# First norm carried into the matmuls, first mixer: compression panels between the dense ones, gates beside the values

## The chip, the cores and the metric

One core of one Trainium2 chip. The metric is the time of one execution on the device in microseconds, median of several runs. One run was also profiled, and all rows below come from it.

## What is computed

Two transformer blocks over 512 tokens of 1024 features, in float32. The change touches only the front of the first block: the first norm and the projections that feed its mixer.

```
h = rms_norm(x, norm_mix_pre)             # x * rsqrt(mean(x*x) + eps) * w, over 1024 features
proj = h @ w_in                           # 1024 -> 2840 columns, split into
rq, rk (256 each), rv, rg (512 each)      # retention: 4 heads, chunks of 128
nq (512), kcm, vcm (128 each)             # sparse attention: queries, and what is compressed
ksl, vsl, kwn, vwn (128 each), ng (24)    # selected and window keys and values, mixing gates
y_ret = silu(rg) * groupnorm(retention(rope(rq), rope(rk), rv))
# compress(): 31 overlapping blocks of 32 tokens, + pos_emb, flattened to 2048
kc = gelu(blocks(kcm) @ cmp_k_w1) @ cmp_k_w2        # 2048 -> 256 -> 64; the same for vc
out = sigmoid(ng)-weighted sum of attention over kc/vc, selected and window keys
x = x + rms_norm(concat(y_ret, out) @ w_out, norm_mix_post)
```

The matrix products are made from split operands: a float32 weight or activation becomes a rounded high part and the remainder, and each product is three matmuls (high by high, low by high, high by low).

## The kernel before

**Panels.** All weights come as panels of 128 x 1024 floats (512 KB), numbered in the order of use. `SP` loads panel p into `raw[p % 4]` as soon as the low part of panel p-4 exists. ScalarE makes the high part (`split`, a copy of 128 x 1024 into `w_hi[p % 2]`, line 1195), VectorE the remainder (`low`, line 1753, into `w_lo[p % 2]`). `split(p)` waits until TensorE has read panel p-2 (`panel_read`), so behind each panel that TensorE finishes there is a chain of one `split` and one `low` before the panel after next can start. `dense` (lines 489 to 491 through `product`) takes one panel: 8 tiles of three matmuls with 512 moving columns, 24 matmuls. `token_major` takes four panels and puts tokens on the partitions: 96 matmuls.

**Order by hand.** Each engine's program is one list, written out by hand and joined by semaphores. In the front TensorE runs: the sums of squares of the norm (`norm_sums`, line 532), the spread of the inverse root (`norm_wide`, line 549), then panels `RET_Q`, `RET_K` (4 dense), `RET_V` (4, token major, 512 wide), `RET_G` (4 dense), `CMP_IN` (2), `NSA_Q` (4), `NSA_K` (2), `NSA_V` (4, token major, 256 wide), `NSA_GATE` (1 panel of 32 stationary columns, 24 matmuls of 512), `CMP_W1` (8 panels, 12 matmuls of 256 each with 62 stationary columns), `CMP_W2` (1). Then the attention part begins: `best_round` (line 646), 18 rounds whose maxima VectorE takes (`largest`, line 2122), and `block_scores` (line 667). The pieces of the retention (`ret_scores`, `ret_values` line 615, `ret_sums` line 621) are put between tiles of dense panels.

**The first norm.** `x` comes in one DMA on ScalarE's queue, behind two others. ScalarE squares the 8 tiles, VectorE adds them up, TensorE sums over partitions, GpSimd takes the power, VectorE spreads it on a diagonal, TensorE widens it, and only then VectorE scales tile after tile (line 1821), ScalarE makes the high part (line 1289) and VectorE the low part (line 1828) for the first dense panel. Later norms of the kernel are "carried": the matmuls run on x times the gain, and the inverse root multiplies the results.

**VectorE's helpers in the front.** `rope_panel` (lines 1953 to 1958, four operations of 128 x 512), `ret_decay` (line 1997), the centring of the values (lines 2023 to 2025), `xg` building for the compression (line 2044, eight operations for each of keys and values), `xg_low` (line 2030), `q_lows` (line 1976), `k_lows` (line 1984). All sit in one queue with `low`.

Of the kernel before, what the change touches and what calls it, by code (L numbers as in the profile page):

```python
# [21 lines left out]
P = 128  # L22
# [12 lines left out]
FF0 = 42  # L35
# [64 lines left out]
CARRIED = ("ffn_pre", "ab", "ffn1", "c", "ffn2")  # L100
# [14 lines left out]

def output_of(panel):

    before = panel - sum(4 for at in (RET_V, NSA_V, AB_V, AB_VB, AB_O) if panel > at)
    return before if panel <= CMP_W1 else before - 2 if panel <= MLA_V else before - 2 - 2 - PAIRS


CMP_O = output_of(CMP_W1)


def bank_at(panel):

    if AB_U <= panel < AB_O:
# [11 lines left out]
def build_in(nc, A, ctx):  # L139
# [25 lines left out]
    with ExitStack() as c:  # L165
# [83 lines left out]
    def table(t, where, name):  # L249
# [4 lines left out]
    consts_in, x_in, first_in, second_in, pos_in = (sem(n) for n in (  # L254
        "consts_in", "x_in", "first_in", "second_in", "pos_in"))
# [5 lines left out]
    gates_turned, cmp_in_ready, cmp_turned, cmp_ready, v_ready = (sem(n) for n in (  # L261
        "gates_turned", "cmp_in_ready", "cmp_turned", "cmp_ready", "v_ready"))
# [34 lines left out]


# [52 lines left out]
    inv_b = tmp[:, 1, :]  # L351
    ADDED = ("ffn_pre", "ab")
# [26 lines left out]
    def _(sp):  # L379
        for n in range(4):  # L380
# [13 lines left out]
    def _(pool):  # L394
# [7 lines left out]
        pool.wait_ge(consts_in, 32)  # L402
        sets = [6]
# [28 lines left out]
        pool.wait_ge(x_in, 32)  # L432
# [53 lines left out]
    def _(pe):  # L486
# [6 lines left out]
        def w(panel, a, b):  # L493
            return w_hi[:, panel % 2, a:b], w_lo[:, panel % 2, a:b]

        def dense(panel, i=None, moving=(h_hi, h_lo), tiles=KD, ready=None, base=0, most=None, between=None, freed=False):
# [298 lines left out]
        pe.wait_ge(consts_in, 32)  # L795
        pe.wait_ge(x_in, 16)
        norm("mix_pre")
        pe.wait_ge(pool_set, 6)
# [17 lines left out]

        def retention_in(panel):
            def between(k):
                if k in ret_work[panel]:
                    part, n = ret_work[panel][k]  # L820
                    part(n)
            return between if panel in ret_work else None

        for panel in range(RET_G, NSA_V):
            dense(panel, between=retention_in(panel))
        pe.wait_ge(ret_p, 16)
        pe.wait_ge(ret_ms, 4)
        token_major(NSA_V, 256)
        o = output_of(NSA_GATE)
        pe.wait_ge(w_lo_ready, NSA_GATE + 1)  # L830
        pe.wait_ge(tile_out, o - 3)
        for k in range(KD):
            last = product(ps[0:32, o % 4, :], w(NSA_GATE, k * 32, (k + 1) * 32), (h_hi[:, k, :], h_lo[:, k, :]),
                           k == 0, k == KD - 1)
        last.then_inc(panel_read, 1)

        def turn_hidden(kv):

            o = CMP_O + 2 * kv
            pe.wait_ge(tile_out, o + 1)  # L840
            for m in range(2):
                last = nc.tensor.transpose(ps[:, (o + 1) % 4, m * 64:m * 64 + 62], ev[0:62, o % 4, m * P:(m + 1) * P],
# [2039 lines left out]
```

## Time and profile before

| | |
|---|---|
| median of 3 runs | 2020.8 us (2019.57 to 2021.36) |
| profiled run | 2019.84 us, of which 2018.1 us is the span from first to last instruction |
| TensorE (PE) busy | 1909.0 us, 95% |
| VectorE (DVE) busy | 1128.6 us, 56% |
| ScalarE (ACT) busy | 725.9 us, 36% |
| chain that ended last | 71% PE, 18% issue, 7% DVE, 2% ACT |
| mean granted TensorE clock | 0.977 |

A PE that is busy is not PE at its peak: matmuls are pipelined, and a row's duration is longer than the distance from one matmul to the next. So the distance between starts is what counts for throughput, and a milestone in the timeline (the start of the first matmul of a panel) is the surest number. Idle time in brackets behind a row is what the engine spent before that instruction, and the name behind the arrow is what released it.

### The profile page before, as it was taken

The page shows a single profiled execution, that of the slowest core. Times are in us where ns is not written, and L with a number is a line of the kernel's source. Part 1 is how long each engine was busy: PE and PEld are TensorE (multiplying, and loading weights), DVE is VectorE, ACT ScalarE, POOL GpSimd, SP SyncE. Part 2 cuts the span into 40 slices and gives each one's busy share as a digit, 9 for nine tenths or more (in the row PEclk, how much of TensorE's full clock was granted, in tenths as well). Part 3 has the DMA queues.
Part 4 walks back from the last instruction along what each step waited for, and adds up shares of the span by engine and source line. Part 5 has one row for each costly group of instructions (what it writes and reads, how often), then busy time and mean ns, then how long its engine had stood idle before and what let it go on. Part 6 is the DMA issues. An engine that isn't in the chain of part 4 may idle for free.

```text
span 2018.1 us, 24723 instructions
## 1 busy us (share of the span) xinstructions
PE 1909.0 (95%) x9036; PEld 1564.7 (78%) x9036; DVE 1128.6 (56%) x1584; ACT 725.9 (36%) x1030; POOL 98.8 (5%) x105
## 2 busy tenths in 40 slices
PE   3998799989999998999899999999999999999997
PEld 2787577778888876777688888888788888888886
DVE  4557564478476576766654434356777554344444
ACT  2326222244243244454432323243444333223232
POOL 1010000020000002000000000001211000000000
PEclk9999699999999998999999999999999999999998
DMA  4213301222333332231133323323111033233333
GB/s 156 81 57 105 104 1 43 84 63 94 96 102 95 94 104 89 82 93 41 53 92 101 94 94 100 98 94 88 58 32 32 22 94 94 94 102 96 94 95 113
DMA packets 47237, 167.74 MB, mean 83 GB/s; under 512 B 5040, under 2 KB 5040, under 8 KB 47024
## 3 DMA queue, kind: packets, MB, share of 16 engines
q1 hardware_dynamic: 44352, 159.40, 25.9%
q10 hardware_dynamic: 2800, 7.19, 1.0%
q8 instruction: 55, 0.90, 0.2%
q14 instruction: 30, 0.25, 0.0%
HBM read 164.47 MB, written 2.10 MB: 83 GB/s over the span
## 4 chain that ended last, share of the span: by engine, by line
PE 71%; issue 18%; DVE 7%; ACT 2%; DMA 1%; POOL 1%; ACTq 0%; POOLq 0%; DVEq 0%
PE ps L489 20%; PE ps L491 20%; PE ps L490 20%; PE ps L781 3%; PE ps L682 2%; DVE w_lo L1753 1%; PE ps L1019 1%; PE ps L646 1%; DMA x_in<-in_x 1%; ACT w_hi L1195 1%; PE ps L753 1%; PE ps L549 1%; PE ps L532 1%; DVE mx L2122 1%; DVE qk_c L2314 0%
## 5 line engine op out<-in xcount | busy, mean ns | idle before, releaser
L1195 ACT ACTIVATE w_hi<-raw 128x1024 fp32r<-128x1024 f32 x297 | 314.3, 1059 | 881.3 <-PE ps L491 880.4
L489 PE MATMUL ps<-h_hi,w_hi 128*128 128x512 f32 x1312 | 525.7, 401 | 17.0 <-DVE h_lo L1845 9.0
L490 PE MATMUL ps<-h_lo,w_hi 128*128 128x512 f32 x1312 | 515.2, 393 | 0.0
L491 PE MATMUL ps<-h_hi,w_lo 128*128 128x512 f32 x1312 | 514.9, 392 | 0.0
L1753 DVE TENSOR_TENSOR w_lo<-raw,w_hi 128x1024 fp32r<-128x1024 f32 x297 | 364.6, 1229 | 191.1 <-ACT w_hi L1195 181.5
L489 PEld LDWEIGHTS ps<-h_hi,w_hi 128*128 128x128 f32 x1312 | 248.2, 189 | 82.9 <-issue 19.8
L490 PEld LDWEIGHTS ps<-h_lo,w_hi 128*128 128x128 f32 x1312 | 248.4, 189 | 53.3 <-issue 2.4
L491 PEld LDWEIGHTS ps<-h_hi,w_lo 128*128 128x128 f32 x1312 | 248.2, 189 | 53.5
L489 PE MATMUL ps<-hid_hi,w_hi 128*128 128x512 f32 x688 | 268.1, 390 | 1.3 <-DVE hid_lo L2233 0.8
L491 PE MATMUL ps<-hid_hi,w_lo 128*128 128x512 f32 x688 | 267.7, 389 | 0.0
L490 PE MATMUL ps<-hid_lo,w_hi 128*128 128x512 f32 x688 | 267.6, 389 | 0.0
L1885 DVE TENSOR_TENSOR x<-x,ps 128x512 f32<-128x512 f32 (+1 forms) x80 | 55.0, 687 | 196.8 <-PE ps L491 196.6
L489 PEld LDWEIGHTS ps<-hid_hi,w_hi 128*128 128x128 f32 x688 | 129.1, 188 | 29.4 <-DVE w_lo L1753 1.4
L491 PEld LDWEIGHTS ps<-hid_hi,w_lo 128*128 128x128 f32 x688 | 129.1, 188 | 26.8
L490 PEld LDWEIGHTS ps<-hid_lo,w_hi 128*128 128x128 f32 x688 | 129.2, 188 | 26.7
L2502 DVE SCALAR_TENSOR_TENSOR ev<-ps,tmp 128x512 f32<-128x512 f32 x64 | 44.3, 692 | 161.4 <-PE ps L491 156.7
L414 POOL TENSOR_TENSOR r<-r,small 128x4 f32<-128x4 f32 x11 | 11.1, 1011 | 1496.1 <-DVE r L1805 1496.1
L781 PEld LDWEIGHTS ps<-mla_v,c_raw 128*128 128x128 f32 x512 | 65.4, 191 | 5.4 <-issue 0.5
L781 PE MATMUL ps<-mla_v,c_raw 128*128 128x65 f32 x512 | 64.0, 268 | 0.0
L1389 ACT ACTIVATE c_raw<-ps 128x512 f32<-128x512 f32 x64 | 38.3, 598 | 67.9 <-PE ps L491 67.8
L1408 ACT ACTIVATE pr<-ps 128x512 f32<-128x512 f32 x48 | 28.1, 597 | 88.4 <-PE ps L672 88.3
L489 PE MATMUL ps<-w_hi,h_hi 128*128 128x512 f32 (+1 forms) x128 | 47.2, 368 | 4.3 <-DVE w_lo L1753 4.3
(354 smaller groups left out, 2278.1 us busy)
## 6 DMA issues: line engine op xcount, KB each, us to landing
raw<-in_panels SPq DMA_DIRECT2D x300, 512.0 KB, 3.6
x_in<-in_x ACTq DMA_DIRECT2D x1, 2048.0 KB, 17.1
x<-in_x ACTq DMA_DIRECT2D x1, 2048.0 KB, 8.4
out<-y SPq DMA_DIRECT2D x8, 256.0 KB, 2.1
first<-in_first ACTq DMA_DIRECT2D x1, 1568.0 KB, 20.4
second<-in_second ACTq DMA_DIRECT2D x1, 512.0 KB, 3.5
small<-in_small ACTq DMA_DIRECT2D x1, 332.0 KB, 5.1
masks<-in_masks ACTq DMA_DIRECT2D x1, 256.0 KB, 6.8
```

The lines of the kernel that those rows point to most:

```text
L489: nc.tensor.matmul(out, a[0], b[0], start=start, stop=False)
L490: nc.tensor.matmul(out, a[0], b[1], start=False, stop=False)
L491: return nc.tensor.matmul(out, a[1], b[0], start=False, stop=stop)
L532: last = nc.tensor.matmul(ps[:, 6, t:t + 1], tile[:, t * P:(t + 1) * P], ones[:, 0:1], start=start and t == 0, stop=stop, skip_group_check ...
L682: last = nc.tensor.matmul(ps[:, 6 + n // 6, n % 6 * 65:n % 6 * 65 + 65], pr[:, m % 4, h * P:(h + 1) * P], v, start=w["kt"] == 0 and n in ( ...
L781: last = nc.tensor.matmul(ps[:, mla_bank(n), t * 65:(t + 1) * 65], mla_pr[:, m % 4, t * P:(t + 1) * P], mla_v[:, kt, n, :], start=kt == 0 ...
L1195: nc.scalar.activation(w_hi[:, panel % 2, :], raw[:, panel % 4, :], ACT.Copy).then_inc(w_hi_ready, 1)
L1389: nc.scalar.activation(mla_pr[:, m % 4, :], ps[:, 4 + m % 2, :], ACT.Exp, scale=96 ** -0.5).then_inc(exp_done, 1)
L1408: nc.scalar.activation(pr[:, m % 4, :], ps[:, 4 + m % 2, :], ACT.Exp, scale=0.125).then_inc(block_exp, 1)
L1753: signal(V.tensor_tensor(w_lo[:, panel % 2, :], raw[:, panel % 4, :], w_hi[:, panel % 2, :].bitcast(F32), ALU.subtract), w_lo_ready, wait= ...
L1885: signal(V.tensor_tensor(x[:, k, :], x[:, k, :], bank, ALU.add), tile_out)
L2502: signal(V.scalar_tensor_tensor(ev[:, k % 4, :], bank, 0.0, inv_b, ALU.max, ALU.mult), tile_out, wait=False)
```

## The change

- The first norm joins the carried ones. `x` comes in 8 DMAs of one tile each on `SP`'s queue, between the first panels; `first` and `masks` move to that queue behind panels 0 to 3. ScalarE and VectorE make high and low part of x times the gain as each tile lands; the squares come afterwards, the sums inside the second dense panel, the widening inside the third. The inverse root is applied by scaling the two rope tables, the copies of the value panels, and with one more VectorE multiply in `CMP_IN`; the gate copy of `RET_G` becomes a multiply.
- A third weight buffer `w_third` for the panels of `CMP_W1` and `CMP_W2`. Each `CMP_W1` panel follows a dense panel; the panels are renumbered, `CMP_IN` comes before `RET_G`, and `NSA_V` comes last, behind `CMP_W2`.
- A compression panel takes 8 matmuls of 256 columns, not 12: high and low parts of `xg` stand side by side as 126 stationary columns, and their sums are added afterwards (`hidden_part`, `hidden_sum`).
- The 24 gate columns ride with the value panels (`V_WIDTH` 288, not 256); panel `NSA_GATE` and its transposes are gone. `silu` runs once over all of `rg`, `sigmoid` on the gate columns.
- Dense outputs of the front use three banks, not four; bank 3 holds the compression sums.

```diff
-RET_Q, RET_K, RET_V, RET_G = 0, 2, 4, 8
-CMP_IN, NSA_Q, NSA_K, NSA_V, NSA_GATE = 12, 14, 18, 20, 24
-CMP_W1, CMP_W2, OUT1 = 25, 33, 34
+RET_Q, RET_K, RET_V, CMP_IN = 0, 2, 4, 8
+RET_G, NSA_Q, NSA_K = (10, 12, 14, 16), (18, 20, 22, 24), 26
+CMP_W1, CMP_W2 = ((11, 13, 15, 17), (19, 21, 23, 25)), 28
+NSA_V, OUT1 = 29, 33
+V_WIDTH = 288
+def buffer_of(panel):
+    if panel >= OUT1:
+        return panel % 2
+    return 2 if panel in THIRD else (FRONT.index(panel) + 1) % 2
@@ SP
+        x_tile(0)
+        first_panel(0)
+        for k in (1, 2, 3):
+            x_tile(k)
+        first_panel(1)
+        for k in (4, 5, 6, 7):
+            x_tile(k)
+        first_panel(2)
+        first_panel(3)
+        sp.dma_start(first[:], A["first"]).then_inc(first_in, 16)
+        sp.dma_start(masks[:], A["masks"]).then_inc(masks_in, 16)
@@ TensorE
-        norm("mix_pre")
-        for panel in range(RET_Q, RET_V):
-            dense(panel, ready=n_lo if panel == RET_Q else None)
-        pe.wait_ge(normed, KD)
+        dense(RET_Q, ready=n_lo)
+        dense(RET_Q + 1, between=sums_at("mix_pre", 4))
+        dense(RET_K, between=wide_at("mix_pre", 1))
+        dense(RET_K + 1)
+        pe.wait_ge(inv_copied, 1)
         token_major(RET_V, 512)
+        def compress(kv, c):
+            panel = CMP_W1[kv][c]
+            pe.wait_ge(w_lo_ready, panel + 1)
+            if c == 0:
+                pe.wait_ge(cmp_in_ready, kv + 1)
+            high, rest = w(panel, 0, PANEL)
+            for kk in range(4):
+                kt, cols = 4 * c + kk, slice(kk * 256, kk * 256 + 256)
+                both = xg[:, kt, :, :].rearrange("p a b -> p (a b)")
+                nc.tensor.matmul(ps[0:126, 3, 0:256], both[:, 0:126], high[:, cols], ...)
+                last = nc.tensor.matmul(ps[0:62, 3, 0:256], xg[:, kt, 0, 0:62], rest[:, cols], ...)
+        dense(CMP_IN, between=retention_in(CMP_IN))
+        dense(CMP_IN + 1, between=retention_in(CMP_IN + 1))
+        for t in range(4):
+            dense(RET_G[t], between=retention_in(RET_G[t]))
+            compress(0, t)
+        dense(NSA_Q[0], between=retention_in(NSA_Q[0], turn=0))
+        compress(1, 0)
+        dense(NSA_Q[1], between=retention_in(NSA_Q[1]))
+        compress(1, 1)
+        dense(NSA_Q[2])
+        compress(1, 2)
+        dense(NSA_Q[3])
+        compress(1, 3)
+        dense(NSA_K, between=turn_second)
+        dense(NSA_K + 1)
         pe.wait_ge(w_lo_ready, CMP_W2 + 1)
+        pe.wait_ge(cmp_split, 2)
...
+        pe.wait_ge(ret_ms, 4)
+        token_major(NSA_V, V_WIDTH)
@@ VectorE, first half of its new list
+        centre(0)
+        ret_decay(0)
+        centre(1)
+        ret_decay(1)
+        centre(2)
+        ret_decay(2)
+        low(10)
+        low(11)
+        centre(3)
+        ret_decay(3)
+        ret_decay(4)
+        compress_in(0)
+        ret_decay(5)
+        low(12)
+        xg_low(0)
+        for m in (6, 7, 8):
+            ret_decay(m)
+        compress_in(1)
+        gate_of(0)
+        low(13)
+        low(14)
+        for m in (9, 10, 11):
+            ret_decay(m)
...
@@ VectorE, its end
+        low(29)
+        q_lows(3)
+        low(30)
+        rope_panel(9, copied(NSA_K + 1))
+        k_lows(0)
+        low(31)
+        dve.wait_ge(panel_read, CMP_W2 + 1)
...
+        low(32)
+        k_lows(1)
+        low(33)
+        low(34)
@@ ScalarE, its end
+        turn_out(NSA_K + 1)
+        k_highs(0)
+        split(31)
+        k_highs(1)
+        split(32)
+        split(33)
+        split(34)
+        by_tokens(NSA_V, ACT.Copy, lambda t: nv[:, t, :, :, 0:64], 256, scale=inverse_column)
+        for t in range(NT):
+            nc.scalar.activation(gates[:, t, :], ps[:, 4 + t, 256:V_WIDTH], ACT.Sigmoid, scale=inverse_column(t)).then_inc(gates_ready, 1)
```

## Rows read from the trace of the kernel before

**Rows 1.** The page's slices: granted TensorE clock in tenths, 40 slices of 50 us.

```profile
PEclk9999699999999998999999999999999999999998
```

**Rows 2.** Busy us (xinstructions) by stretch: PE, PEld, DVE, ACT, POOL; clock, DMA, GB/s.

```profile
10.00:20.00 10.00, 0.00 (x0) 0.00 (x0) 0.82 (x2) 1.15 (x2) 0.00 (x0) 1.00 1.05 418
...
220.00:240.00 20.00, 11.91 (x46) 8.63 (x46) 10.10 (x31) 2.68 (x5) 0.00 (x0) 0.50 0.23 77
```

**Rows 3.** The chain that ended last, in order of time: start us, us, what.

```profile
1.68 17.09 DMA x_in<-in_x
...
24.86 3.56 PE ps L532 x16
```

**Rows 4.** Timeline from the first squares to full pace: start us, us, instruction, [idle before].

```profile
23.22 0.63 ACT L1237 ACTIVATE sq<-x_in 128x512 f32<-128x512 f32 x1 [0.17 <-DVE tmp L1799]
...
28.44 0.16 DVE L1805 TENSOR_SCALAR r<-ps 128x4 f32<-128x4 f32 x1 [3.73 <-PE ps L532]
...
35.09 0.76 PE L489 MATMUL ps<-h_hi,w_hi 128*128 128x512 f32 x1 [2.39 <-DVE h_lo L1828]
...
39.15 0.50 PE L489 MATMUL ps<-h_hi,w_hi 128*128 128x512 f32 x1
```

**Rows 5.** Timeline of TensorE: first matmuls of RET_V and RET_G, then the stall.

```profile
61.29 0.39 PE L489 MATMUL ps<-w_hi,h_hi 128*128 128x512 f32 x1
...
83.05 0.39 PE L489 MATMUL ps<-h_hi,w_hi 128*128 128x512 f32 x1
...
92.98 0.36 PE L489 MATMUL ps<-rq_hi,rk_hi 128*128 128x256 f32 x1 [3.74 <-DVE ret_pr L1997]
...
93.68 0.63 PE L490 MATMUL ps<-h_lo,w_hi 128*128 128x512 f32 x1
...
96.67 0.55 PE L491 MATMUL ps<-h_hi,w_lo 128*128 128x512 f32 x1
```

**Rows 6.** Timeline from NSA_V to the attention part: first matmuls of its stages.

```profile
175.17 0.28 PE L489 MATMUL ps<-w_hi,h_hi 128*128 128x256 f32 x1
...
185.41 0.39 PE L489 MATMUL ps<-w_hi,h_hi 128*128 128x256 f32 x1 [4.33 <-DVE w_lo L1753]
...
192.76 0.39 PE L489 MATMUL ps<-h_hi,w_hi 128*32 128x512 f32 x1
...
198.28 0.28 PE L489 MATMUL ps<-w_hi,xg_hi 128*62 128x256 f32 x1
198.40 0.28 PE L490 MATMUL ps<-w_lo,xg_hi 128*62 128x256 f32 x1
...
230.77 0.37 PE L646 MATMUL ps<-kcs,qs 128*128 128x32 f32 x1 [6.31 <-DVE r L2100]
...
232.13 0.29 DVE L2122 TENSOR_REDUCE mx<-ps 128x4 f32<-128x128 f32 x1 [1.50 <-PE ps L648]
...
247.10 0.78 PE L667 MATMUL ps<-qs,kcs 128*128 128x512 f32 x1
```

**Rows 7.** Groups by line and shape, VectorE 83 to 250 us, ScalarE 0 to 250 us.

```profile
L1753 DVE TENSOR_TENSOR w_lo<-raw,w_hi 128x1024 fp32r<-128x1024 f32 x27 | 33.0, 1225 | 41.0 <-ACT w_hi L1195 40.8
L2122 DVE TENSOR_REDUCE mx<-ps 128x1 f32<-128x512 f32 x16 | 10.9, 692 | 2.9 <-PE ps L650 2.9
L2044 DVE TENSOR_TENSOR xg_f<-ev,small 64x248 f32<-64x248 f32 x16 | 9.1, 609 | 0.1
L1976 DVE TENSOR_TENSOR ql<-tmp,qs 64x512 fp32r<-64x512 f32 x8 | 5.5, 683 | 0.1
...
L1195 ACT ACTIVATE w_hi<-raw 128x1024 fp32r<-128x1024 f32 x36 | 38.0, 1058 | 103.2 <-PE ps L491 102.5 <-DMA raw<-in_panels 0.7
```

**Rows 8.** DMA issues by line: count, KB each, median us from issue to landing.

```profile
raw<-in_panels SPq DMA_DIRECT2D x300, 512.0 KB, 3.6
...
x<-in_x ACTq DMA_DIRECT2D x1, 2048.0 KB, 8.4
...
small<-in_small ACTq DMA_DIRECT2D x1, 332.0 KB, 5.1
```

More of the change, by code:

```diff
@@ L29 @@
 HALF_SWAP = [*range(16, 32), *range(16)]
-RET_Q, RET_K, RET_V, RET_G = 0, 2, 4, 8
-CMP_IN, NSA_Q, NSA_K, NSA_V, NSA_GATE = 12, 14, 18, 20, 24
-CMP_W1, CMP_W2, OUT1 = 25, 33, 34
-FF0 = 42
+RET_Q, RET_K, RET_V, CMP_IN = 0, 2, 4, 8
[3 more added lines that the diff above has]
+V_WIDTH = 288
+THIRD = CMP_W1[0] + CMP_W1[1] + (CMP_W2,)
+FRONT = [panel for panel in range(OUT1) if panel not in THIRD]
+FRONT_OUT = [panel for panel in FRONT if not (RET_V <= panel < RET_V + 4 or panel >= NSA_V)]
+RET_SLOTS = (CMP_IN, CMP_IN + 1, *RET_G, *NSA_Q[:2])
+FF0 = OUT1 + 8
 FF0_CHUNKS = [8, 8, 6]
@@ L351, in build_in @@
     inv_b = tmp[:, 1, :]
+    inv_mix = tmp[:, 3, :]
     ADDED = ("ffn_pre", "ab")
@@ L818, in between, with retention_in @@
+        def retention_in(panel, turn=None):
+            work = ret_work[RET_SLOTS.index(panel)]
             def between(k):
-                if k in ret_work[panel]:
-                    part, n = ret_work[panel][k]
+                if k in work:
+                    part, n = work[k]
                     part(n)
[L822 to L835, printed above, removed]
-        def turn_hidden(kv):
-            o = CMP_O + 2 * kv
-            pe.wait_ge(tile_out, o + 1)
+                if turn is not None and k == 6:
+                    turn_hidden(turn)
@@ new lines, in _ @@
+        split(10)
+        split(11)
+        turn_out(CMP_IN)
+        split(12)
+        turn_out(CMP_IN + 1)
+        xg_highs(0)
+        for t in range(4):
+            turn_out(RET_G[t])
+            if t < 3:
+                ret_out(t)
+                split(13 + 2 * t)
+                split(14 + 2 * t)
+        hidden_part(0)
+        split(19)
+        split(20)
+        hidden_open(0)
+        xg_highs(1)
+        turn_out(NSA_Q[0])
+        ret_out(3)
+        split(21)
+        split(22)
@@ L1366, in _ @@
+        turn_out(NSA_K + 1)
         k_highs(0)
+        split(31)
         k_highs(1)
-        for c in range(4):
-            split(NSA_V + c + 2)
-        by_tokens(NSA_V, ACT.Copy, lambda t: nv[:, t, :, :, 0:64], 256)
-        step(NSA_GATE, ACT.Sigmoid, rows=32)
-        for kv in range(2):
-            panel, o = CMP_W1 + 4 * kv, CMP_O + 2 * kv
-            for c in range(4):
-                split(panel + c + 2)
-            out(o, ACT.Gelu_apprx_tanh, panel + 4, cols=256, rows=62)
-            out(o + 1, ACT.Copy, kv + 1, cols=P, ready=cmp_turned)
@@ new lines, in _ @@
+        ret_mean(0)
+        gate_of(1)
+        low(15)
+        low(16)
+        for m in (12, 13):
+            ret_decay(m)
+        ret_mean(1)
+        gate_of(2)
+        low(17)
+        low(18)
+        for m in (14, 15):
+            ret_decay(m)
+        ret_mean(2)
+        gate_of(3)
+        hidden_sum(0)
+        low(19)
+        low(20)
+        xg_low(1)
+        hidden_split(0)
+        rope_panel(4, copied(NSA_Q[0]))
+        low(21)
+        low(22)
+        ret_mean(3)
+        rope_panel(5, copied(NSA_Q[1]))
@@ new lines, in _ @@
+        low(23)
+        low(24)
+        dve.wait_ge(ret_pv, 16)
+        q_lows(0)
+        rope_panel(6, copied(NSA_Q[2]))
+        low(25)
+        low(26)
+        q_lows(1)
+        rope_panel(7, copied(NSA_Q[3]))
+        hidden_sum(1)
+        low(27)
+        low(28)
+        q_lows(2)
+        dve.wait_ge(pool_set, 19)
+        hidden_split(1)
+        rope_panel(8, copied(NSA_K))
+        low(29)
[3 more added lines that the diff above has]
+        k_lows(0)
@@ L2703, in lay_panels, with place @@
[L2703 to L2710 removed]
+    front = np.zeros((OUT1, P, PANEL), np.float32)
+    def place(at, panels):
+        front[list(at)] = panels
```

414 lines of the change are left out of this document (209 added, 205 removed).

## The prediction, made before the changed kernel was timed

> **What bounds the kernel now.** The page first: TensorE is busy for 95% of the span, and its granted clock dips in few slices [rows 1]: the first, the second, the fourth and the fifth (10, 50, 150 and 200 us in), then one or two far behind. All but the far ones lie in what the change touches. The stretches show why: up to 20 us TensorE does nothing while the DMAs run at 418 GB/s, and from 220 to 240 it is busy 11.91 of 20 us at half clock [rows 2]. The chain in order of time then names the first cause: the path begins with the 17.09 us DMA of `x`, and the sums on TensorE (3.56 us) stand behind it [rows 3]. The timeline gives the milestones. The first dense matmul starts at 35.09, full pace comes at 39.15 [rows 4]. RET_V starts at 61.29 and ends at 83.05; then a stall of 3.74 us on a VectorE product, and behind it a stretch at the lower of the two clocks (1.2, not 2.4 GHz): from 93.68 to 96.67 seven steps of 0.43 us, where full pace is 0.227 [rows 5]. NSA_V starts at 175.17 and is cut by a stall of 4.33 us on `w_lo`, the gate panel takes 192.76 to 198.28, the compression and its tail 198.28 to 230.77, and `block_scores` starts at 247.10 [rows 6]. I take this last as the end of the front: what follows has the same work, so the change is worth what this milestone moves, plus nothing behind it.
>
> **Part 1, the carried norm.** Removed: the wait for all of `x`, the squares and sums ahead of the first matmul, the scaling pass. Added: x times gain split as tiles land. From the DMA rows, 512 KB land in 3.6 us and 2048 KB in 8.4 [rows 8], so 2.0 us fixed and 3.2 us per MB on one queue. The last tile has 3.1 MB before and with it: 0.75 + 2.0 + 9.6 = 12.4 us, panel 0 at 5.2, panel 1 at 9.3. The first split waits for `small` (issued at 0.75, 5.1 us [rows 8]): 6 us. ScalarE: eight splits at 0.65 and two panels at 1.06 [rows 7], done at 13.2. VectorE: eight at 0.70 (as other 128x512 operations [rows 7]) and two `low` at 1.23, done at 15.3; the last tile keeps TensorE to 16.5. It starts at the lower clock as before (4.1 us from first matmul to full pace [rows 4]), which VectorE's pace half hides. Then five tiles (3.4 us), a wait for VectorE's sum (0.8 a tile behind 15.3, as now [rows 4], so 20.5), the 16 sum matmuls. Those took 3.56 us cold [rows 3]; at full clock about half, 1.7; I take 1.7 and keep 3.6 for the range. The widening costs 0.9 on TensorE; the power on GpSimd lies beside tiles. So 20.5 + 1.7 + the panel's last three tiles 2.0 + two more panels 10.9 + 0.9 = 36.0; with a semaphore's time between, RET_V starts at 36.2. What must be in time: `low(4)` (needs the scaled rope tables, the first `rope_panel`, and `split(4)` behind panel 2): about 33. Cover 3 us. The tables in `first` have 6.2 MB before them, about 21 us, needed at 27; if that cover goes, it costs the excess. RET_V is the same 21.76: it ends at 58.0 where it ended at 83.05. **Minus 25.1.**
>
> **Part 2, RET_V to NSA_V.** Now 92.12 us (83.05 to 175.17). The stall of 3.74 goes: VectorE's new order puts each `ret_decay` behind the first centring, not behind all four; with it goes the slow stretch, 8 matmuls by 0.20, 1.6. Remains 86.8. Added on TensorE: 8 compression panels of 8 matmuls by 0.118 (the distance now between such matmuls [rows 6]), 7.6; transposes 0.7; CMP_W2, 18 matmuls at 0.12, 2.2. Its weights hide in the third buffer: `split` and `low` (1.06 + 1.23 [rows 7]) of a compression panel need only the compression panel before, a whole dense panel earlier. Next I walked ScalarE's and VectorE's lists against that clock. VectorE per query panel: two `low` 2.46, a rope of four operations 2.75, `q_lows` 1.38 [rows 7], 6.6 us, against TensorE's 5.46 + 0.95 = 6.4: even, and it enters with some 2 us in hand. ScalarE needs 5.2. The place that gives way is RET_G's second panel: `compress_in(1)` (8 by 0.609 [rows 7] plus the multiply, 5.3), `gate_of(0)`, `low(13)`, `low(14)` stand ahead of `ret_decay(9)`, and `ret_scores(11)` waits for it. My walk has it ready 33.8 after RET_V's end, wanted at 31.8: a stall of 2.0, and a slow stretch of 1.6 behind it (the two stalls above 3.7 us were each followed by one; for 2 us it is open, bounds 0 and 1.7). 86.8 + 7.6 + 0.7 + 2.2 + 3.6 = 100.9: NSA_V starts at 158.9, now 175.17 with compression and CMP_W2 still to come.
>
> **Part 3, NSA_V last.** 96 matmuls of 288 columns: between 0.12 at 256 and 0.227 at 512, by columns 0.134, 12.9 us. The present stall of 4.33 is `k_highs` and `k_lows` ahead of `split` and `low`. In the new order `low(31)` still waits behind `rope_panel(9)` and `k_lows(0)`, ready 1.4 late, and `low(32)` behind the key preparation (some 15 small operations, which lie in the 6.31 us wait before 230.77 today [rows 6]), 1.5 late. 15.8 in all: it ends at 174.7. The gate panel (5.5), the compression's own stretch of 22 us with its split-low chain per 2.8 us panel, and the 6.31 us wait before 230.77 [rows 6] are gone from the path; all of the key preparation now lies under NSA_V. New at the end: VectorE does `low(34)` (behind `split(34)`, which waits for NSA_V's last matmul) before it takes the first maximum: 2.4 us after the end, 177.1. `sigmoid` with its table load is done about 4 us after the end and first wanted 17 us after. Two more table loads of 1.3 us (the compression's two gelus now stand either side of the silu) lie in ScalarE's slack.
>
> **Part 4, the rounds.** First maximum to `block_scores` takes 14.97 now (232.13 to 247.10), 16 maxima of 692 ns with 2.9 us of waits for TensorE, at half clock [rows 2, 6, 7]. After NSA_V TensorE is warm, then idles 2.4 us and works a third of the time. I take it as slow as now; at full clock the waits would go and 2.5 be saved. `block_scores` at 192.1.
>
> **Sum.** 247.10 - 192.1 = 55.0. The profiled execution took 2019.84 (span 2018.1): 1964.8. The median of the runs is 0.96 above the profiled one: **1965.8**. Behind the front, one panel less is loaded, buffers and banks alternate as before: 0.
>
> A rule of the Trainium skill speaks against the split load. "DMA: Bandwidth & Descriptors", section "Bandwidth", asks for DMAs of at least 1 MiB, and gives a fixed 2 us for each smaller one. Taken one by one, its 2.0 plus bytes over 436 GB/s make an estimate of 21 us for the eight tiles. The trace has the fixed 2.0 us too, but with several DMAs in flight it shows 418 GB/s [rows 2].
>
> **Rivals.** *Tiles that don't overlap.* If each DMA of the queue waited for the one before, eight tiles (2.8 each by the fit above) and two panels (3.6) would end at 30; the first dense panel ends at 32, not 16.5: +15.5, 1981. Against: rows 2. *The wait moves to VectorE.* One VectorE queue holds `low` for both kinds of panel. If its list is late in each of the eight doubled slots by one `split` and `low` chain, 2.3 us, that is +18, 1984. For: the balance 6.6 against 6.4 and the stall already found; against: VectorE is busy 56%, and its slack grows in the slots of RET_G. *Warm to the end.* No slow stretch behind the 2 us stall, rounds at full clock, no stall in NSA_V: -1.6 - 2.5 - 2.9, 1959. *Nothing.* The front is hidden by something later: against it stands that the chain runs through it without a gap. *Slower.* The clock stays at its lower level through the front because TensorE starts early with pauses: 0.20 us for each matmul of 512 columns, and some 480 are in it, +96 from 1966, 2062. It decides beyond 275 slow matmuls, 117 us at that level. For: 220 to 240 sat at 0.50 [rows 2]; against: each slow stretch ended some 4 us after work resumed [rows 4, 5].
>
> **How the numbers follow.** Forecast 0.64 (its own range 1960 to 1973: sums at cold price +2, small waits of up to 5 that my walk missed, and half of the warm case), warm to the end 0.11, VectorE late 0.15, no overlap 0.05, nothing 0.02, slower 0.03. The range reaches to the warm case and into the VectorE case: 1957 to 1979, which leaves out 0.19: no overlap, nothing, slower, and the far half of VectorE late. This kernel's measurement can tell 0.2% (4 us) from no change. Faster 0.95, same 0.02, slower 0.03.
>
> **What would show it.** First dense matmul near 9 us, RET_V near 36 and done near 58; a stall near 90 on a `ret_pr` product; no panel of compression waiting for `w_lo`; VectorE never behind by over 2 us in NSA_Q; NSA_V from 159 to 175 with two stalls on `w_lo`; first maximum at 177, `block_scores` at 192. Wrong if tiles land after 15 us, if a `w_lo` wait over 1 us stands before dense query panels, or if anything behind `block_scores` differs by over 2 us.

## The result and the profile after

| | before | after |
|---|---|---|
| median of 4 runs, us | 2020.75 (2019.57 to 2021.36) | 1961.06 (1960.54 to 1961.79) |
| profiled run, us (its span) | 2019.84 (2018.1) | 1961.36 (1959.6) |
| mean granted TensorE clock | 0.977 | 0.983 |

The ratio is 0.9706, 95% interval 0.9689 to 0.9722: the change takes 3% away. The predicted 1965.8 lies 4.7 us above the median, the whole range below the time before.

The page of after: busy time by engine, and the granted clock in 40 slices of 49 us.

```profile
PE 1889.0 (96%) x8976; PEld 1552.2 (79%) x8976; DVE 1124.8 (57%) x1578; ACT 728.6 (37%) x1032; POOL 97.4 (5%) x106
...
PEclk9998999999999989999999999999999999999998
```

In the front, [rows 1] has a single low slice, 6 tenths from 200 us on. Here that slice is gone, and the lowest one of the front is at 8 tenths, from 147 to 196 us. The timeline of after, engines TensorE and ScalarE, gives the milestones of the start (start us, us, instruction, idle before and its releaser).

```profile
4.58 1.28 ACT L1303 ACT_TABLE_LOAD   x1 [4.58 <-DMA x_in<-in_x]
...
9.06 0.77 PE L541 MATMUL ps<-h_hi,w_hi 128*128 128x512 f32 x1 [9.06 <-DVE w_lo L1854]
...
14.32 0.44 PE L541 MATMUL ps<-h_hi,w_hi 128*128 128x512 f32 x1
...
20.53 0.95 PE L586 MATMUL ps<-small,tmp 128*128 128x1 f32 x8
21.34 1.03 PE L586 MATMUL ps<-small,sq 128*128 128x1 f32 x8
...
36.17 0.39 PE L541 MATMUL ps<-w_hi,h_hi 128*128 128x512 f32 x1
...
57.94 0.39 PE L541 MATMUL ps<-h_hi,w_hi 128*128 128x512 f32 x1
```

The first dense matmul starts at 9.06 where it was 35.09 [rows 4], and RET_V at 36.17 where it was 61.29 [rows 5]. The sums of squares now take 1.7 us (20.53 to the next dense matmul at 22.23) in the middle of dense work at full clock, not 3.56 alone [rows 3]. The DMAs deliver from the start; the stretch with its busy us by engine, clock, DMA share and GB/s, and the issues of `x_in`:

```profile
10.00:20.00 10.00, 10.00 (x36) 8.00 (x35) 9.06 (x14) 8.00 (x14) 0.00 (x0) 1.00 1.02 411
...
x_in<-in_x SPq DMA_DIRECT2D x8, 256.0 KB, 5.8
```

TensorE works all of those 10 us where it did nothing [rows 2], at almost the same 411 GB/s. The clock column has 1.00 for this stretch, but the matmuls do not run at full pace in all of it: up to 14.32 they start 0.43 us apart, and only behind that 0.23. So for the start of the kernel the lower clock is read from the distance between matmuls. Next the middle and the end of the front, timeline of after:

```profile
91.73 0.30 PE L541 MATMUL ps<-rq_hi,rk_hi 128*128 128x128 f32 x1 [1.47 <-DVE ret_pr L2091]
...
156.79 0.38 PE L541 MATMUL ps<-w_hi,h_hi 128*128 128x288 f32 x1
...
164.10 0.40 PE L541 MATMUL ps<-w_hi,h_hi 128*128 128x288 f32 x1 [0.75 <-DVE w_lo L1854]
...
168.26 0.40 PE L541 MATMUL ps<-w_hi,h_hi 128*128 128x288 f32 x1 [0.72 <-DVE w_lo L1854]
...
171.53 0.18 PE L700 MATMUL ps<-kcs,qs 128*128 128x32 f32 x1
...
174.02 1.64 DVE L2273 TENSOR_REDUCE mx<-ps 128x4 f32<-128x128 f32 x3
...
174.36 0.49 PE L700 MATMUL ps<-ks,qs 128*128 128x512 f32 x1 [1.75 <-DVE mx L2273]
...
188.62 0.78 PE L721 MATMUL ps<-qs,kcs 128*128 128x512 f32 x1
```

The 3.74 us stall [rows 5] has become one of 1.47, the 4.33 before `w_lo` [rows 6] two of 0.75 and 0.72, and the 6.31 us wait for the compressed keys [rows 6] is gone. `block_scores` starts at 188.62 where it started at 247.10 [rows 6]: 58.48 us. Behind it 1770.98 us are left, and before it was 2018.1 - 247.10 = 1771.00. How alike the two are is in part chance, as the table below has 1767.3 to 1772.2 in this place; but a wait for `by_token` that both kernels have lies 102.27 us behind the milestone here and 102.33 there. So the change lies in the front.

### The profile page after: what moved, and what is told of

Same layout as the page of the kernel before. It is cut to its first block, busy times and chain, and to the rows that moved or that the text cites. A ratio compares the mean times of both kernels' runs of the same rounds, so it can differ in the third digit from the quotient of the medians.

```text
span 1959.6 us, 24595 instructions
## 1 busy us (share of the span) xinstructions
PE 1889.0 (96%) x8976; PEld 1552.2 (79%) x8976; DVE 1124.8 (57%) x1578; ACT 728.6 (37%) x1032; POOL 97.4 (5%) x106
## 4 chain that ended last, share of the span: by engine, by line
PE 72%; issue 19%; DVE 7%; ACT 2%; POOL 1%; DMA 0%; POOLq 0%; DVEq 0%; ACTq 0%
PE ps L541 20%; PE ps L542 20%; PE ps L543 20%; PE ps L835 3%; PE ps L736 2%; DVE w_lo L1854 1%; PE ps L1077 1%; PE ps L700 1%; ACT w_hi L1253 1%; PE ps L807 1%; PE ps L603 1%; PE ps L586 1%; DVE qk_c L2466 0%; DVE mx L2273 0%; PE ps L1037 0%
## 5 line engine op out<-in xcount | busy, mean ns | idle before, releaser
L1253 ACT ACTIVATE w_hi<-raw 128x1024 fp32r<-128x1024 f32 x287 | 303.8, 1059 | 821.0 <-PE ps L543 820.8
L1854 DVE TENSOR_TENSOR w_lo<-raw,w_hi 128x1024 fp32r<-128x1024 f32 x287 | 352.5, 1229 | 143.4 <-ACT w_hi L1253 141.9
L541 PEld LDWEIGHTS ps<-h_hi,w_hi 128*128 128x128 f32 x1304 | 247.7, 190 | 83.4 <-issue 25.1
L2351 DVE TENSOR_REDUCE mla_mx<-ps 128x1 f32<-128x512 f32 x64 | 41.2, 685 | 13.3 <-PE ps L807 12.8
```

The source lines that it names most:

```text
L541: nc.tensor.matmul(out, a[0], b[0], start=start, stop=False)
L1253: nc.scalar.activation(w_high(panel), raw[:, panel % 4, :], ACT.Copy).then_inc(w_hi_ready, 1)
L1854: signal(V.tensor_tensor(w_low(panel), raw[:, panel % 4, :], w_high(panel).bitcast(F32), ALU.subtract), w_lo_ready, wait=False)
L2351: signal(V.tensor_reduce(mla_mx[:, n % 2, t:t + 1], ps[:, 2 + t % 2, :], AX.X, ALU.max), mx_done, wait=False)
```

## The experiments

Each kernel is the one after with the edit shown, but for the last, which is the one before with an edit. Times of milestones are starts in the timeline of its profiled execution: RET_V, NSA_V, the first round (NSA_V done), `block_scores`, and the span left behind that.

| kernel | median us | ratio to before, 95% | RET_V | NSA_V | round | blocks | rest |
|---|---|---|---|---|---|---|---|
| after | 1961.06 | 0.9689 to 0.9722 | 36.17 | 156.79 | 171.53 | 188.62 | 1770.98 |
| one_x_dma | 1971.32 | 0.9749 to 0.9788 | 46.98 | 167.59 | 182.31 | 199.03 | 1770.37 |
| norm_first | 1977.98 | 0.9777 to 0.9810 | 51.12 | 171.68 | 186.43 | 203.87 | 1770.53 |
| centres_first | 1968.07 | 0.9725 to 0.9758 | 36.18 | 163.83 | 178.55 | 196.00 | 1770.20 |
| twelve | 1964.25 | 0.9710 to 0.9742 | 35.72 | 159.47 | 174.18 | 191.47 | 1770.73 |
| vec_extra | 1965.82 | 0.9712 to 0.9756 | 37.21 | 161.57 | 176.66 | 193.87 | 1767.33 |
| early_decay | 1960.28 | 0.9680 to 0.9716 | 37.30 | 156.75 | 171.49 | 188.30 | 1772.20 |
| late_low | 1958.37 | 0.9671 to 0.9708 | 36.36 | 156.89 | 171.63 | 186.67 | 1769.93 |
| late_low_warm | 1955.39 | 0.9662 to 0.9713 | 35.98 | 156.52 | 171.26 | 184.44 | 1767.86 |
| keys_order | 1962.17 | 0.9688 to 0.9726 | 36.52 | 158.63 | 171.36 | 189.14 | 1771.16 |
| joined | 1955.91 | 0.9664 to 0.9697 | 37.23 | 156.09 | 168.82 | 183.04 | 1767.56 |
| values_256 | 1961.10 | 0.9691 to 0.9726 | 36.25 | 156.84 | 171.29 | 188.39 | 1771.21 |
| before_warm | 2017.01 | 0.9968 to 0.9987 | | | | 248.24 | 1768.76 |

### What the start is worth

**One DMA for x** on ScalarE's queue, as before, with `masks` ahead of it and `first` behind it; all else as after.

```diff
-        x_tile(0)
-        first_panel(0)
...
+        for n in range(4):
+            first_panel(n)
@@ ScalarE
+        act.dma_start(masks[:], A["masks"]).then_inc(masks_in, 16)
+        act.dma_start(x_in0[:], A["x"].rearrange("k p s -> p k s")).then_inc(x_tile_in[0], 16)
+        act.dma_start(first[:], A["first"]).then_inc(first_in, 16)
```

> Undoes one part: x comes again in one DMA behind small and masks on ScalarE's queue, with the four panels on SP's; the norm stays carried. If the start is bound by the arrival of x: x lands near 18.8 us as in the kernel before (last tile by 12 now), the first dense panel ends near 25.5 instead of 16.5, and RET_V starts near 45, 9 us later than the 36.2 of the changed kernel; the whole is 9 us slower (1970). Rival, the sums and the pow chain set RET_V's start whatever the arrival: under 3 us slower.

TensorE's first matmul and the DMA of `x`, in its timeline and its issues:

```profile
20.54 0.77 PE L532 MATMUL ps<-h_hi,w_hi 128*128 128x512 f32 x1 [20.54 <-DVE w_lo L1848]
...
x_in<-in_x ACTq DMA_DIRECT2D x1, 2048.0 KB, 14.3
```

The one DMA is in flight together with four panels and lands after 14.3 us. The 8.4 us of [rows 8] are not its measure: that row is a later load of `x`, 345 us into the kernel before, while the front's own DMA of `x` took 17.09 us there [rows 3], also beside four panels. RET_V comes 10.81 us later, `block_scores` 10.41, the median 10.3. So the eight tiles, with `masks` and `first` moved behind them, are worth about 10 us here. The Trainium skill's rule of at least 1 MiB per DMA ("DMA: Bandwidth & Descriptors", section "Bandwidth") did not hold against them: eight of 256 KB, in flight together with the panels, kept 411 GB/s, and the consumer can start on the first. The fixed 2 us that the prediction names beside this rule stands in another section of that page, "Anatomy of one DMA — SWDGE (gpsimd) path", and holds there for a DMA of any size.

**The norm ahead of the matmuls**, with the tile DMAs kept.

```diff
-CARRIED = ("mix_pre", "ffn_pre", "ab", "ffn1", "c", "ffn2")
+CARRIED = ("ffn_pre", "ab", "ffn1", "c", "ffn2")
@@ TensorE
+        norm("mix_pre")
@@ VectorE
-            carry_low("mix_pre", k)
...
+        norm_split_of("mix_pre")
```

> Undoes one part: the first norm is complete before the first dense matmul (squares, sums, pow, widening, scaling), the tiles still come in eight DMAs. The multiplies by the inverse root stay as multiplies by one. In the kernel before, RET_V started 36.6 us after the last square; the last square now ends near 13.5, so RET_V starts near 50, +14 us, and the whole takes 1975. With one_x_dma's 9 that gives 23 of the 25 us that the front gained. Rival: most of the gain was the arrival of x, then this costs under 5 us.

TensorE's start in its timeline:

```profile
14.66 1.84 PE L586 MATMUL ps<-small,tmp 128*128 128x1 f32 x8 [14.66 <-DVE tmp L1889]
16.36 1.84 PE L586 MATMUL ps<-small,sq 128*128 128x1 f32 x8
20.43 2.08 PE L603 MATMUL ps<-tmp,small 128*128 128x512 f32 x2 [2.22 <-DVE tmp L1901]
24.90 0.77 PE L541 MATMUL ps<-h_hi,w_hi 128*128 128x512 f32 x1 [2.40 <-DVE h_lo L1918]
```

RET_V is 14.95 us later. The sums take 3.6 us at the start's clock, as before [rows 3], and the two waits of 2.22 and 2.40 are the round trips that the carried norm puts under dense tiles. 14.95 and 10.81, each undone alone, make 25.8, against 25.12 that the start gained as a whole (61.29 - 36.17): these two parts account for it, though no run undoes both at once.

### What sets the pace of the middle

**All centrings ahead of the first `ret_decay`**, VectorE's order before.

```diff
         centre(0)
-        ret_decay(0)
         centre(1)
-        ret_decay(1)
         centre(2)
+        centre(3)
+        ret_decay(0)
+        ret_decay(1)
         ret_decay(2)
         low(10)
         low(11)
-        centre(3)
```

> Undoes one part: VectorE centres all four value tiles before the first ret_decay, as in the kernel before. The stall of 3.1 to 3.7 us on ret_pr returns near 64 us on TensorE. If a stall of that length always brings a slow stretch, 1.6 us more: the whole is 4.7 to 5.3 us slower. If the clock only falls after longer or other pauses: 3.1 to 3.7. Rival: VectorE catches up later and the wait was hidden, 0.

The stall in its timeline, and two stretches with their busy us and clock:

```profile
67.87 0.36 PE L541 MATMUL ps<-rq_hi,rk_hi 128*128 128x256 f32 x1 [3.68 <-DVE ret_pr L2091]
...
68.53 0.50 PE L542 MATMUL ps<-h_lo,w_hi 128*128 128x512 f32 x1
68.83 0.63 PE L543 MATMUL ps<-h_hi,w_lo 128*128 128x512 f32 x1
69.25 0.63 PE L541 MATMUL ps<-h_hi,w_hi 128*128 128x512 f32 x1
...
97.25 0.30 PE L541 MATMUL ps<-rq_hi,rk_hi 128*128 128x128 f32 x1 [1.47 <-DVE ret_pr L2091]
...
68.00:76.00 8.00, 8.00 (x29) 6.03 (x30) 3.17 (x5) 2.49 (x3) 0.00 (x0) 0.79 0.17 54
98.00:104.00 6.00, 6.00 (x28) 4.95 (x27) 1.37 (x4) 3.16 (x5) 0.00 (x0) 0.72 0.35 128
```

The stall of [rows 5] is back, 3.68 us, with a slow stretch of 8 matmuls behind it (from 68.83, at 1.2 GHz). Stall and stretch put the 1.47 us stall that the kernel after has too 5.5 us later (97.25, not 91.73), and NSA_V comes 7.04 late. The other 1.5 is a second slow stretch, behind that 1.47 us stall, where the kernel after has none. So the order is worth 5.5 us, and a further 1.5 came by the clock.

**Twelve matmuls for each compression panel**, not eight: high and low part of `xg` apart, 62 columns each.

```diff
-                nc.tensor.matmul(ps[0:126, 3, 0:256], both[:, 0:126], high[:, cols], ...)
-                last = nc.tensor.matmul(ps[0:62, 3, 0:256], xg[:, kt, 0, 0:62], rest[:, cols], ...)
+                last = product(ps[0:62, 3, 0:256], (xg[:, kt, 0, 0:62], xg[:, kt, 1, 0:62]), (high[:, cols], rest[:, cols]), ...)
```

> Undoes one part: a compression panel takes 12 matmuls of 62 stationary columns again, not 8 with high and low side by side. 32 more matmuls by 0.118 us are 3.8 us if TensorE's own work sets the time between RET_V and NSA_V; the whole is 3.8 slower, spread evenly (0.47 for each of the eight panels). Rival, VectorE's list sets the time in the query slots (6.6 us against 6.4): then the four panels there cost nothing, 1.9 or less.

RET_V to NSA_V takes 123.75, not 120.62: 3.1 us for 32 matmuls, 0.10 each; the stall on `ret_pr` shrank by 0.5 (1.47 to 0.97), so the matmuls themselves cost 3.6. Work on TensorE is paid almost in full: it bounds the middle, not the chains of `split` and `low`.

**More VectorE work** where it is busiest: eight operations by 0.68 us in the slots of `NSA_Q`, 5.4 us in all.

```diff
+        for _ in range(2):
+            link(V.tensor_tensor(xg_f[:, 0:8, :], xg_f[:, 0:8, :], xg_f[:, 8:16, :], ALU.max))
```

> Adds two VectorE operations of 0.5 KB rows (128x496, about 0.68 us each) behind each of the four query ropes, 5.4 us in all; their result is not used. If VectorE has slack in the query slots (no w_lo wait of TensorE before NSA_V in the changed kernel's trace): at most 1 us slower before NSA_V, and some of it from the two w_lo stalls of 0.75 there growing. If VectorE's demand (6.6 us a slot) is level with TensorE's 6.4, it is 5.4 minus a cover of about 2: 3 to 4 us slower.

First the stretch 140 to 160 of after, then that of vec_extra and its two new waits:

```profile
140.00:160.00 20.00, 20.00 (x112) 17.27 (x111) 17.96 (x31) 16.65 (x25) 0.00 (x0) 1.00 0.41 131
```

```profile
140.00:160.00 20.00, 18.48 (x87) 14.63 (x85) 18.67 (x33) 15.67 (x23) 0.00 (x0) 1.00 0.42 146
...
145.58 0.38 PE L889 MATMUL ps<-w_third,xg 128*126 128x256 f32 x1 [0.31 <-DVE w_third L1854]
...
153.02 0.33 PE L902 MATMUL ps<-small,cmp_h 62*128 62x62 f32 x2 [1.21 <-ACT cmp_h L1411]
```

In the kernel after TensorE is busy all of the 20 us, though VectorE is at 17.96. 5.4 us more of VectorE cost 1.5 directly (0.31 + 1.21). NSA_V less RET_V grew by 3.7. Of this 1.5 is a slow stretch behind the 1.47 us stall (clock 0.72 from 94 to 100), which is far ahead of the added work, and 2.2 fell in the query slots, 0.7 more than the two waits. The first `w_lo` stall in NSA_V grew too, from 0.75 to 1.13. So the 5.4 us cost about 2.6 in the front. RET_V came 1.04 late as well, by a slow stretch at 23 to 26 us. Both stretches lie ahead of the added work. The median, 4.8 above that of after, holds such stretches and the scatter of its runs (1963.42 to 1970.0), so it is no measure of the edit. My balance of 6.6 against 6.4 was roughly right in size, but some 3 us of slack stand behind it: the rival with 18 us is out.

**One `ret_decay` earlier**, between `low(13)` and `low(14)`.

```diff
         low(13)
+        ret_decay(9)
         low(14)
-        for m in (9, 10, 11):
+        for m in (10, 11):
```

> One swap on VectorE: ret_decay(9) before low(14). The stall of 1.47 us on ret_pr at 91.7 goes (ret_pr is ready 1.2 us earlier), nothing is late next since low(14) is wanted at 97. Minus 1.2 to 1.5 us, 1960. Rival: the work queued behind makes it up, 0.

VectorE's queue ahead of the stall in the kernel after, from its timeline:

```profile
83.61 4.38 DVE L2141 TENSOR_TENSOR xg_f<-ev,small 64x248 f32<-64x248 f32 x8
88.02 0.69 DVE L2146 TENSOR_TENSOR rg<-ev,tmp 128x512 f32<-128x512 f32 x1
88.75 1.22 DVE L1854 TENSOR_TENSOR w_third<-raw,w_third 128x1024 fp32r<-128x1024 f32 x1
89.89 1.22 DVE L1854 TENSOR_TENSOR w_lo<-raw,w_hi 128x1024 fp32r<-128x1024 f32 x1
91.03 0.88 DVE L2091 TENSOR_TENSOR ret_pr<-ps,first 128x384 f32<-128x384 f32 x2
```

That is the queue which the prediction walked through. With the edit the stall is 0.33, and RET_V to NSA_V takes 119.45, 1.17 less. In the profile that gain is hidden; its start, from the timeline:

```profile
19.98 1.05 PE L586 MATMUL ps<-small,tmp 128*128 128x1 f32 x8 [0.20 <-DVE tmp L1891]
...
22.11 0.39 PE L542 MATMUL ps<-h_lo,w_hi 128*128 128x512 f32 x1
...
22.65 0.63 PE L541 MATMUL ps<-h_hi,w_hi 128*128 128x512 f32 x1
23.08 0.63 PE L542 MATMUL ps<-h_lo,w_hi 128*128 128x512 f32 x1
```

TensorE paused 0.20 us before the sums, the matmuls from 22.65 to 25.21 ran at the lower clock, and RET_V came 1.13 late. The kernels vec_extra and joined have the same stretch. The edit lies far behind this place, so the stretch is not its work. The median is 0.8 under that of after, inside both intervals.

### What sets the pace of the end

**`low(34)` behind the maxima of the rounds**, and the same with one spare matmul of 512 columns into an unused bank behind each round.

```diff
-        low(34)
@@ VectorE, behind the rounds
+        low(34)
```

> One move on VectorE: low(34) goes behind the maxima of the first two units. The first maximum is then at 172.0, not 174.0, and TensorE no longer pauses 1.75 us after NSA_V. If the clock fell because of that pause, it stays at 2.4 GHz through the rounds and block_scores starts 4 to 5 us earlier (184); if TensorE's light load in the rounds makes it fall anyway, it starts 2.0 earlier (186.6), and the whole is 2.0 faster.

```diff
                 best_round(u, r)
+                nc.tensor.matmul(ps[:, 0, :], qs[0][:, 0, 0, :], h_hi[:, 0, :], start=True, stop=True)
```

> late_low, and behind each of the 18 rounds one matmul of 512 columns into a bank that nobody reads, to keep TensorE loaded. If the load decides the clock: it stays at 2.4 GHz, VectorE's 16 maxima run back to back, block_scores starts near 184 and its first blocks run at full pace: 4 to 5 us faster than the changed kernel. If the added matmuls only take time (0.43 us each at 1.2 GHz, 18 of them): 3 to 5 us slower than late_low.

The same two stretches of late_low and then of late_low_warm: busy us by engine, clock.

```profile
176.00:182.00 6.00, 4.89 (x20) 3.00 (x19) 4.42 (x9) 1.82 (x5) 0.00 (x0) 0.50 0.00 0
182.00:188.00 6.00, 5.77 (x15) 3.16 (x16) 4.91 (x9) 0.00 (x0) 0.00 (x0) 0.50 0.01 3
```

```profile
176.00:182.00 6.00, 5.29 (x30) 3.25 (x29) 5.29 (x11) 1.46 (x2) 0.00 (x0) 1.00 0.01 3
182.00:188.00 6.00, 5.89 (x37) 4.08 (x36) 5.42 (x9) 1.44 (x3) 0.00 (x0) 1.00 0.02 8
```

late_low takes 15.04 us from the first round to `block_scores`, after 17.09: the 2.05 that VectorE no longer spends first. The clock still falls to 1.2 GHz, at about 175.1 (174.8 in the kernel after), although the first maximum now comes 0.8 us behind the first round, not 2.5. With the spare matmuls it stays at 2.4 GHz and the same part takes 13.18. Behind it the first dense matmuls no longer run slow: the wait for `by_token` comes 101.03 us after `block_scores`, and 101.8 to 102.5 in all kernels without spare matmuls. So the pause ahead of the rounds was not what took the clock down; it falls in the rounds themselves, and further matmuls there prevent it. Up to `by_token` the profiled executions differ by 3.04 us (288.51 and 285.47), of which 0.37 was there before the first round, so the spare matmuls are worth 2.67. The medians differ by 2.98, but one of the four runs of late_low_warm took 1962.57, longer than any of late_low, and the intervals of the two overlap. What the last column of the table has beyond that is scatter: vec_extra has 1767.33 with no spare matmul.

**The same spare matmul in the kernel before.**

> The kernel before, with one spare matmul of 512 columns behind each of the first 18 rounds. There TensorE enters the rounds at 1.2 GHz after a pause of 6.3 us. If load brings the clock back within about 4 us: the rounds take near 13.5 instead of 15.0, the blocks start at full pace, 4 to 5 us faster in all. If the spare matmuls at 1.2 GHz (0.43 each) delay the maxima so that nothing is won: within 1 us.

The stretch 232 to 248 of before and then of before_warm:

```profile
232.00:248.00 16.00, 14.31 (x44) 7.79 (x44) 12.25 (x20) 0.00 (x0) 0.00 (x0) 0.50 0.00 0
```

```profile
232.00:248.00 16.00, 14.92 (x67) 8.96 (x67) 11.18 (x21) 0.00 (x0) 0.00 (x0) 0.78 0.01 4
```

There the engine enters the rounds at the lower clock, behind the long wait of [rows 6]; the granted clock rises at 239, so only half the rounds gain: first round to `block_scores` 15.87 us, not 16.33, and from there to `by_token` 101.02, not 102.33. That is 1.8; the medians differ by 3.8, and the ratio's interval, 0.9968 to 0.9987, is clear of 1. Where the other 2 come from the profile does not show: it reaches NSA_V 1.2 us later than that of before (176.38), by a longer slow stretch behind the 3.74 us stall. The spare matmuls are a gain of their own, which does not need the change.

**Keys ahead of `k_lows(0)`.**

```diff
         rope_panel(9, copied(NSA_K + 1))
-        k_lows(0)
         low(31)
+        k_lows(0)
+        low(32)
         dve.wait_ge(panel_read, CMP_W2 + 1)
...
-        low(32)
         k_lows(1)
```

> VectorE's order at the end of the front: low(31) before k_lows(0), and low(32) before the key preparation. Both stalls of TensorE on w_lo in NSA_V (0.75 and 0.72 us) go; the key preparation ends near 169, still ahead of NSA_V's end at 170.0. Minus 1.5 us if these two are the late ones; 0 if ScalarE's split, behind k_highs, sets them.

What VectorE does at NSA_V's end, and TensorE's wait, in its timeline:

```profile
170.84 1.39 DVE L2082 TENSOR_TENSOR ks<-tmp,ks 64x512 fp32r<-64x512 f32 x2
172.26 2.36 DVE L1854 TENSOR_TENSOR w_lo<-raw,w_hi 128x1024 fp32r<-128x1024 f32 x2
174.54 1.64 DVE L2273 TENSOR_REDUCE mx<-ps 128x4 f32<-128x128 f32 x3
...
174.88 0.50 PE L700 MATMUL ps<-ks,qs 128*128 128x512 f32 x1 [2.44 <-DVE mx L2273]
```

Both `w_lo` stalls are gone and NSA_V takes 12.73 us, not 14.74. But the operations are still there: two `low` now stand ahead of the first maximum, which comes 3.18 us after NSA_V's end, not 2.49. Of 2.0 us, 1.3 are left at `block_scores` (30.51 from NSA_V, not 31.83). The expected 1.5 us less do not show in the median, which is 1.1 above that of after, inside both intervals: this profile again has a slow stretch behind the 1.47 us stall, and starts NSA_V 1.8 later.

**Value panels without the gate columns.** `V_WIDTH` is 256; the mixing gates are left out and read columns that hold something else.

```diff
-V_WIDTH = 288
+V_WIDTH = 256
```

> Leaves out the 24 gate columns (the value panels are 256 wide again, and the gates are taken from whatever the bank holds), to price them. By TensorE's work NSA_V is 96 by 0.014, 1.3 us, shorter. If the split and low chain sets the pace instead (2.5 us a panel against 2.9), part of it comes back as longer w_lo stalls: 0.5 to 1.3 us in all. The gate panel cost 5.5 us in the kernel before, so 4 or more are saved either way.

RET_V to the first round takes 135.04, not 135.36. The matmuls are shorter, and the two stalls on `w_lo` longer, 1.34 and 1.01: of about 1.2 us that the matmuls save, the stalls take back 0.9. So NSA_V's pace is mostly that of VectorE's list, of its `low` and the key work between them, which keys_order moves. The gate columns cost 0.3 us there, and nothing that the medians can tell (1961.10 against 1961.06), where the gate panel they replace took 5.5 [rows 6].

**Four edits joined**: `ret_decay(9)` ahead of both `low(13)` and `low(14)` (one place further than in early_decay), keys_order, late_low and the spare matmuls.

> Four edits together: ret_decay(9) before low(13) and low(14) (1.2 to 1.5), the keys' order (1.5), low(34) behind the first maxima and a spare matmul behind each of the first 18 rounds (7.3 together, measured). If they add up as parts of one path: 59 + 10 us under the first kernel, near 1950. If the late ones only uncover each other: 1953 to 1955, no better than the spare matmuls alone.

No wait for `ret_pr` or `w_lo` is left; the first round starts at 168.82, `block_scores` at 183.04, 5.6 us earlier than after, and `by_token` 6.8 earlier. The profiled execution has the shortest span of all, 1950.6, though it has a slow stretch at the start (22.59 to 25.15). The median, 1955.91 of 1951.97 to 1957.1, is 5.2 under that of after and not told apart from the 1955.39 of late_low_warm, so the two further edits add nothing that the medians show. These two are the fastest kernels of the study.

## Why the prediction was right, and where it was off

**Start.** By its milestones: first matmul predicted near 9, measured 9.06; sums 20.5 and 20.53; their price 1.7 and 1.7; RET_V 36.2 and 36.17; end of RET_V 58.0 and 57.94. Not every step behind these numbers was right, and that they meet so closely is in part luck:

- The fit of 2.0 us and 3.2 us per MB rests on the 8.4 us of a DMA far behind the front; the front's own 2048 KB took 17.09 [rows 3].
- The first split was put at 6 us by `small` alone. It came at 5.88, behind a tile of `x` (4.5) and a table load of 1.28 that the forecast had not put there.
- The forecast lets VectorE hold TensorE up, to 16.5 in the first panel and to 20.5 before the sums. In the kernel after TensorE waited for neither: VectorE had its low parts done at 14.6 and its sum at 19.7. The 12 slow steps at the start, up to 14.32, carried TensorE to 17.1 and, with five tiles of 0.68, to 20.53. Where the start had only 6 slow steps (early_decay, joined), the wait for the sum did appear, at 0.20 and 0.23 us.
- The reading of [rows 1] was wrong: the row has one low slice, the fifth. The low stretches at 93 and at 185 us stand only in finer windows, and the slow start not even there, as the clock column has 1.00 for it.

The choice of the warm price over the cold 3.56 was right because the sums now follow dense tiles; norm_first has 3.56 with the sums alone, after 1.7 with them inside. one_x_dma and norm_first show that tiles and carried norm are the two causes. The rival *tiles that don't overlap* is out: the last tile of `x` was split at 12.8.

**Middle.** The queue walk had the product for `ret_scores(11)` ready 33.8 us after RET_V's end; it was 33.8 (91.73 - 57.94). TensorE asked for it 32.3 after, not 31.8, as a wait of 0.52 us that I had missed (60 us in, on a copy of the values by ScalarE) had held it up. So the stall was 1.47, not 2.0. The mis-sized term is the slow stretch behind it, 1.6 in the sum, 0 in this execution; its bounds were 0 and 1.7, and both ends occur. In sum 98.85 us where I had 100.9. For a stall of 1.47 us a slow stretch cost 1.5 where it came (vec_extra, keys_order, centres_first).

**End.** The step on NSA_V named the right two stalls on `low(31)` and `low(32)` and gave them 2.9 us. The matmuls alone take 12.73 (keys_order and joined, where no stall is left), close to my 12.9; so the two stalls, 1.47 as listed, cost 2.0 with what is lost around them. As values_256 shows, matmuls and stalls are not terms to be sized apart: VectorE's list, with the key work between its `low`, sets 14.5 to 14.7 whatever the columns, and my walk had it 1.1 too long (15.8). The first maximum came 2.49 after NSA_V's end (predicted 2.4), the rounds took 14.60 (14.97) at half clock. These four terms, 2.05 + 1.06 + 0.37 less 0.09, and 0.06 at the start make the 3.45 of the 3.48 us by which `block_scores` came early. That nothing changes behind it held to 0.06 us at `by_token`. Of the two further table loads that I expected there is one (six up to 177 us, where the kernel before has five up to 231), and the profile's chain passes through those at 4.58 and at 146.10 us, so not all of them lie in slack. The last 1.3 of the 4.7 us by which the median came early is scatter: I put the median 0.96 above the profiled execution, as in the kernel before, and it lies 0.30 below.

**Other rivals.** *The wait moves to VectorE*: vec_extra shows about 2.6 us for 5.4 added; no dense query panel waits for `w_lo`. *Warm to the end* happened in part: no slow stretch in the middle, half of the NSA_V stalls, but not the rounds. My reason for the rounds, that TensorE idles 2.4 us and then works a third of the time, joined two causes; late_low and late_low_warm part them, and the pause is not the one. *Slower* is out: in the front the clock was low only to 14.3, and from 174.8 to 191.9.

**What stays open.** centres_first, twelve, vec_extra and values_256 size single pieces: 5.5 for the order of centring, 3.6 for the 126 columns, 0.3 paid for the gate columns. With the start's 25.1 that is about 34 of 58.5. The rest is the compression's own stretch of 22 us, the 6.31 us wait and the gate panel leaving the path, less the compression's matmuls between dense panels and what NSA_V costs in its new place. This is read from the milestones; no run puts the compression back behind NSA_V alone, so the share of each of these is not shown. Nor is it settled why the same short stall is followed by a slow stretch in one execution and not in another.

## What to carry to other kernels

Add up milestones on the bounding engine and walk the hand-written queue of the next busiest one, operation by operation: the ready time of the critical product came out within 0.1 us, while what the clock does after a short stall could only be given as a bound. Removing a stall by reordering one queue moves its work behind something else; look who waits there (keys_order kept 1.3 of 2.0 us). Where TensorE must wait through a lightly loaded stretch, a few spare matmuls may cost less than the lower clock, there and in what follows.

## What the hardware showed unexpectedly

- The stall of 3.7 us on `ret_pr` was followed by a slow stretch wherever it stood (before, before_warm, centres_first), one of 1.47 us in 3 of 9 profiled executions (centres_first, vec_extra, keys_order, not in after, one_x_dma, norm_first, late_low, late_low_warm, values_256), and in early_decay, joined and vec_extra some 3 us at the lower clock followed the sums (22 to 26 us), while after ran through the same place at full clock. In early_decay and joined a pause of 0.2 us stands before the sums. These three are also the ones in which the lower clock of the start ended soonest (6 or 7 slow steps, in the others of the same start 9 to 13). Each such stretch costs 1 to 3 us, so milestones of like kernels differ by that much. The Trainium skill ("TensorE: Matmul & The Clock Gate", section "What's actually happening") says that the chip judges activity at times not tied to the program, so that one kernel meets the change at different points; the 3 of 9 agree with that.
- Spare work on the busiest engine made the kernel faster: with it TensorE ran the rounds at 1.00, without it at 0.50, and the clock stayed low for 2 to 3 us behind the start of `block_scores` (late_low: to 188.7, after: to 191.9).
- One DMA of 2048 KB took 8.4 us at 345 us in the kernel before [rows 8], 14.3 beside four panels (one_x_dma) and 17.09 beside four panels in the kernel before [rows 3]. What else is in flight fits the first difference; why the last two differ by 2.8 is not shown.
